# Four layers on one core: the second layer's second-half inputs and its gate z computed with the moving operand of both halves of x at once

## The reference

```python
proj = rmsnorm(x, norm_g) @ w_in
xc, zc, qd, kd, vd, zd, a_pre, b_pre = split_cols(proj, OD_SIZES)   # 1024 columns each
xconv = causal_dwconv(xc, conv_c_w) + conv_c_b                      # 4 taps along the tokens
yc = rg_lru(xconv, gate_w, gate_b, lam) * silu(zc)                  # gated linear scan
q, k, v = split(silu(causal_dwconv(concat(qd, kd, vd), conv_d_w)))  # 8 heads of 128
od = gated_delta_chunkwise(l2norm(q), l2norm(k), v, beta, g)        # needs a triangular inverse per head
yd = rmsnorm(od, onorm_g) * silu(zd)
x = x + concat(yc, yd) @ w_out
```

## Time and profile before

| | |
|---|---|
| median of 3 runs | 1913.81 us (1913.79 to 1914.02) |
| the profiled execution's own time | 1913.21 us |
| its span, first to last instruction | 1911.3 us |
| busy: PE, PEld, DVE, ACT, POOL | 1901.8, 1636.2, 1219.0, 1012.4, 170.1 us |
| mean granted TensorE clock | 0.999 of full speed |

### The profile page before, as it was taken

How to read it: one execution, slowest core, us unless ns; L and a number is a source line. 1 busy time by engine, 2 the same in 40 slices (tenths; PEclk the granted TensorE clock), 3 DMA queues, 4 the chain that set the end, 5 groups by cost and what they waited for, 6 DMA issues and landing times.

```text
span 1911.3 us, 26221 instructions
## 1 busy us (share of the span) xinstructions
PE 1901.8 (100%) x10370; PEld 1636.2 (86%) x10370; DVE 1219.0 (64%) x1688; ACT 1012.4 (53%) x1574; POOL 170.1 (9%) x142
## 2 busy tenths in 40 slices
PE   9999999999999999999999999999999999999998
PEld 7888888888889998898888888888888888888886
DVE  6655655555566887687557888645555778754553
ACT  7434445664557765764543345556454344446643
POOL 0000000110011111100001211000000111100110
PEclk9999999999999999999999999999999999999999
DMA  9555545545554444444565554554555555555453
GB/s 351 193 178 187 176 158 187 170 165 183 179 180 157 157 151 161 149 147 163 178 198 190 191 178 166 183 176 158 181 179 188 190 186 174 164 185 171 162 199 133
DMA packets 95033, 340.25 MB, mean 178 GB/s; under 512 B 10704, under 2 KB 11472, under 8 KB 94784
## 3 DMA queue, kind: packets, MB, share of 16 engines
q1 hardware_dynamic: 93536, 333.92, 52.4%
q0 software_dynamic: 944, 3.61, 0.6%
q10 hardware_dynamic: 432, 1.06, 0.1%
HBM read 336.44 MB, written 2.10 MB: 177 GB/s over the span
## 4 chain that ended last, share of the span: by engine, by line
PE 100%; ACT 0%; DVE 0%; issue 0%
PE ACC L736 18%; PE ACC L738 18%; PE ACC L737 18%; PE ACC L741 9%; PE ACC L744 9%; PE ACC L743 5%; PE ACC L742 5%; PE ACC L749 2%; PE ACC L750 2%; PE ACC L751 2%; PE PM L852 1%; PE PM L867 1%; PE PM L905 1%; PE PM L889 1%; PE PM L890 1%; PE PM L888 1%
## 5 line engine op out<-in xcount | busy, mean ns | idle before, releaser
L1441 DVE TENSOR_TENSOR WL<-RAW,WH 128x1024 fp32r<-128x1024 f32 (+1 forms) x624 | 791.8, 1284 | 534.3 <-ACT WH L1075 533.1
L1075 ACT ACTIVATE WH<-RAW 128x1024 fp32r<-128x1024 f32 (+1 forms) x626 | 650.7, 1052 | 508.9 <-PE ACC L738 264.9
L736 PE MATMUL ACC<-WH,XHL 128*128 128x512 f32 x1012 | 402.3, 397 | 0.0
L738 PE MATMUL ACC<-WH,XHL 128*128 128x512 f32 x1012 | 394.3, 390 | 0.0
L737 PE MATMUL ACC<-WL,XHL 128*128 128x512 f32 x1012 | 394.0, 389 | 0.0
L741 PE MATMUL ACC<-XHL,WH 128*128 128x512 f32 x768 | 307.9, 401 | 0.1
L744 PE MATMUL ACC<-XHL,WH 128*128 128x512 f32 x768 | 303.8, 396 | 0.0
L738 PEld LDWEIGHTS ACC<-WH,XHL 128*128 128x128 f32 x1012 | 190.0, 188 | 40.1
L737 PEld LDWEIGHTS ACC<-WL,XHL 128*128 128x128 f32 x1012 | 190.2, 188 | 38.6
L736 PEld LDWEIGHTS ACC<-WH,XHL 128*128 128x128 f32 x1012 | 190.1, 188 | 38.3
L743 PE MATMUL ACC<-XHL,WL 128*128 128x256 f32 x768 | 213.7, 278 | 0.0
(11 more groups left out here) (368 smaller groups left out, 2367.4 us busy)
## 6 DMA issues: line engine op xcount, KB each, us to landing
RAW<-in_w SPq DMA_DIRECT2D x621, 512.0 KB, 3.3
X<-in_x SPq DMA_DIRECT2D x4, 512.0 KB, 11.8
RAW<-in_w SPq DMA_DIRECT2D x6, 256.0 KB, 4.8
Y<-in_xT SPq DMA_DIRECT2D x2, 512.0 KB, 10.1
S<-in_bias POOLq DMA_DIRECT2D x8, 128.0 KB, 2.6
S<-in_od_gate_w POOLq DMA_DIRECT2D x1, 1024.0 KB, 6.1
S<-in_final_norm POOLq DMA_DIRECT2D x1, 1024.0 KB, 7.5
out<-Y SPq DMA_DIRECT2D x2, 512.0 KB, 2.6
```

Source lines behind the costliest of these rows:

```text
L736: e.matmul(o, th, hi[:, kk, :], start=f, stop=False)
L738: m = e.matmul(o, tl, hi[:, kk, :], start=False, stop=l)
L1075: e.activation(hi, src, ACT.Copy).then_inc(s_hi)
L1441: e.tensor_tensor(lo, src, hi.bitcast(F32), ALU.subtract).then_inc(s_lo)
```

## The change

It makes five feat jobs of the second layer wide: qd, kd and vd of the second half (slots 25 to 48) join the "sum" kind, and zc becomes four jobs of kind "zc" whose evacuation is a reduction and a multiplication on DVE. The convolution chains of summed inputs from the third on move: "copied" to 2, "taps" to 3 and "silu" to 4 pieces after the job's end. The sigmoid, exp and tanh steps of the scan come one slot earlier, all eight roots at slot 81. The two silu evacuations of zd come four and two pieces later. gate_c and split_c follow the four zc jobs.

```diff
-SUMMED = (("qd", 0), ("kd", 0), ("xc", 0), ("xc", 1))
+SUMMED = (("qd", 0), ("kd", 0), ("qd", 1), ("kd", 1), ("vd", 1), ("xc", 0), ("xc", 1))
...
-    both(1, "zc", w, 1024, "feat", "zc")
+    wide(1, "zc", w, 1024, "zc")
...
+        for b, late in ((0, 4), (1, 2)):
+            ENDS[LAST[J_OF[1, "zd", b]] + late] = ENDS.pop(LAST[J_OF[1, "zd", b]])
...
-                    at, late = conv_ends(c, i), 0 if CONV[c] in SUMMED else i
-                    put(at + 1 + late, "copied", (c, i))
-                    put(at + 2 + 2 * late, "taps", (c, i))
+                    at = conv_ends(c, i)
+                    after = (1 + i, 2 + 2 * i, 3 + 2 * i) if CONV[c] not in SUMMED else (1, 2, 3) if c < 2 else (2, 3, 4)
+                    put(at + after[0], "copied", (c, i))
+                    put(at + after[1], "taps", (c, i))
                     if c < 6:
-                        put(at + 3 + 2 * late, "silu", (c, i))
+                        put(at + after[2], "silu", (c, i))
...
-                put(b1 + 74 + n // 2, "gate_lru", n, 1)
-                put(b1 + 78 + n // 2, "decay_lru", n)
-                put(b1 + 82 + n // 4, "root_lru", n)
+                put(b1 + 73 + n // 2, "gate_lru", n, 1)
+                put(b1 + 77 + n // 2, "decay_lru", n)
+                put(b1 + 81, "root_lru", n)
...
-                    put((b1 + 92, L(1, "zc", 1) + 1)[b] + i, "gate_c", (b, i))
-                    put((b1 + 93, L(1, "zc", 1) + 2)[b] + i, "split_c", (b, i))
+                    at = L(1, "zc", 2 * b + i) + ((5, 3), (2, 1))[b][i]
+                    put(at, "gate_c", (b, i))
+                    put(at + 1 + (b == 0), "split_c", (b, i))
...
-                e.wait_ge(s_evD, at_D(1, "zc", b) - 1 + i)
+                e.wait_ge(s_evD, at_D(1, "zc", 2 * b + i))
...
                 elif J.kind == "zc":
+                    z = two(ZC[:, 512 * (J.b % 2):512 * (J.b % 2) + 512])
                     e.wait_ge(s_mm, p + 1)
-                    if J.b:
-                        e.wait_ge(s_zg, 2)
-                    for i in range(2):
-                        e.tensor_tensor(two(ZC[:, 512 * i:512 * i + 512]), two(acc[i]), row2, ALU.mult).then_inc(s_evD)
+                    if J.b > 1:
+                        e.wait_ge(s_zg, J.b - 1)
+                    e.tensor_reduce(z, halves_of(j), AX, ALU.add).then_inc(s_evD)
+                    e.wait_ge(s_evD, D_AT[j] - 1)
+                    e.tensor_tensor(z, z, row2, ALU.mult).then_inc(s_evD)
```

## The result

| | before | after |
|---|---|---|
| median, us | 1913.81 | 1923.7 (1923.3 to 1924.8) |
| ratio, 95% interval | | 1.0053 [1.0042, 1.0064] |
| profiled execution, own time / span | 1913.2 / 1911.3 | 1924.8 / 1922.4 |

The change makes the kernel 9.9 us slower. I had said 4.7 us slower, 1918.5, with a range from 1910 to 1922: the side was right, the size half of what came, and the time lies above the range.

What follows compares the result with a forecast made beforehand. PE was taken as the bound, always busy, with DVE a second bound where work is added. -3.75 of pace + 7.0 before slot 50 + 1.6 at zc = +4.8 us; predicted 1918.5, range 1910 to 1922.

Steps and rivals of the forecast that it cites:

- The pace: Forty pieces in slots 25 to 48 and 81 to 96: fewer matmuls save 0.094 us each, -3.75 us in all.
- DVE before slot 50: Slots 28 to 47: 10.6 us more before level_x against a margin of 5.9, so PE waits 7.0 us.
- the collision: Slot 28: v's taps (vd) right after a reduction meet POOL's multiplication, 1.0 us; 1.0 taken for all collisions.
- ACT's wait for the clears: Half 0's inverse: POOL's multiplication of slot 36 comes ahead of its clears, delaying ACT's copy; 2.0 us, ends 0 and 2.8.
- What a wait costs: Before slot 50: PE's wait counted at its length, 10.6 - 5.9 + 2.25 = 7.0 us.
- zd's evacuation: ACT's moved silu of zd: two table loads saved, two added at slot 32; net nothing, ACT waiting for DVE anyway.
- zc on DVE: Slots 84 to 98: 3.6 us more on DVE against a margin of 2.9; PE waits 1.6 us at the first solve.
- B: Rival: no new wait of PE, extra work vanishes in DVE's lag, only pace counts: 1910.1 us; chance 0.23.
- C: Rival: half the extra DVE work falls into DVE's existing waits, PE waits some 4 us: about 1914; chance 0.20.
- D: Rival: the matmuls saved bring nothing, up to the whole -3.75 us goes, waits alone give 1922; chance 0.05.
- E: Rival: the later chains, meant to spare ACT waits for POOL, cost or give nothing; no chance stated.
- The gate weights: Later taps and earlier gate products use some 7 of 18 us to spare: no cost.

Runs made afterwards that it cites:

- vd_only: The kernel before with only v's second half as wide pieces, its chain 2, 3 and 4 slots behind each job: 1913.3 us, ratio 0.9997.
- early_zd: Changed kernel with the LRU's gates and decays a slot earlier and zd's second half evacuated at its last piece, slot 80: 1923.7 us.
- no_q: Changed kernel with the second halves of q, k and v as feat pieces again; zc wide and the other moves kept: 1916.4 us.
- chain_now: Changed kernel with copied, taps and silu of summed jobs back at 1, 2 and 3 slots after the job's end: 1930.2 us.
- q_only: The kernel before with only the second halves of q, k and v wide and their chains a piece later: 1921.2 us.
- clears_first: Changed kernel with GpSimd's three clears for half 0's inverse put ahead of its multiplication for slot 36: 1922.2 us.
- order2: Changed kernel with taps and silu of v's second half a slot later and norm_sq in slot 45 instead of 46: 1925.7 us.
- filled: Changed kernel with eight extra matmuls (1.8 us), their results unread, where PE waits at norm_sum of slot 49: 1923.9 us.
- zd_home: Changed kernel with zd's second half evacuated at slot 80 again, two ScalarE table loads more: 1928.2 us.
- zc_pool: The kernel before with zc wide, zd, gates and decays as in early_zd, and zc's product moved from DVE to GpSimd: 1914.8 us.
- zc_late: zc_pool with zc's last evacuation one slot later, behind the last subtraction of half 1's inverse: 1914.8 us.
- vd_zc_late: zc_late with v's second half wide as well: 1914.1 us, ratio 1.0001 to the kernel before.
- wait_added: The kernel before with two extra ScalarE copies (2.2 us) ahead of its copies for the last part of half 1's inverse: 1915.8 us.
- qd_wide: The kernel before with, of q, k and v, only q's second half wide, and zc wide with old slots for zd, LRU and roots: 1923.6 us.

## Why the prediction was wrong

*The pace: right.* I had 0.094 us a piece; vd_only shows 0.091, and where nothing waits the changed kernel gains 0.08 to 0.09 a slot (slots 36 to 45, 87 to 97).

*DVE before slot 50: right in kind, 0.8 short.* ACT's copies end at 698.16 + 1.73 = 699.89, which is 11.4 us later than in the kernel before once the shift of 0.9 is taken off; my sum was 10.6. The terms one by one: reductions 1.22, and the six taps of slot 47 took 2.44 right before the last part, as said. At slot 28 the taps took 3.48 us for 2.45, the collision of 1.0 as said:
```profile
623.86 3.48 DVE L1698 SCALAR_TENSOR_TENSOR S<-S,VC 128x255 f32<-128x255 f32 x6
...
624.09 1.40 POOL L1977 TENSOR_TENSOR S<-S,C 128x512 f32<-128x512 f32 x1 [12.00 <-DVE S L1476]
```
The multiplications of slots 36, 40 and 44 each hit a small step of the inverse:
```profile
658.72 1.34 DVE L1796 TENSOR_TENSOR SC<-SC,VC 128x256 f32<-128x256 f32 x1
...
674.71 1.32 DVE L1806 TENSOR_TENSOR SC<-SC 128x56 f32<-128x56 f32 x1
```
That is 1.3 us for 0.43 and, twice, for 0.23 to 0.25 (the next of its kind, at 676.57). All four are 4.1; with the 1.9 taken off for slot 40 as before, 2.2, where I had 1.0. Each of them cost 0.9 to 1.1; the count of 1.0 for all four, which I had named and not taken, gives 2.1. ACT's wait for the clears was 2.25 for 2.0. PE's loss at slots 30 to 34 was 3.4 for my 3.3 (2.4 of it as listed idle time).

*What a wait costs: wrong.* The step reads "PE waits 10.6 - 5.9 + 2.25 = 7.0 us" and goes into the sum as 7.0. I counted a wait at its length. Here PE's granted clock fell to its lower level (1.2 instead of 2.4 GHz) behind two waits of four. Slot 51 is 6.8 us late where my sum gives 4.75: 0.8 from DVE, 1.2 from level_x reached late at the lower clock. Behind the wait at slot 85 another 1.1 (slots 85 and 86 begin 3.99 us apart, for 2.88). My sum had no term for this.

*zd's evacuation: wrong, and left out.* "Net nothing, and in each place ACT waits for DVE anyway" is the step that failed. I asked what the two slots do to ACT's table loads, and not who waits for the accumulator; and that zc's jobs are half as long, so that the accumulator is asked for four pieces earlier, I did not see. It costs 2.0 us of wait and the 1.1 of clock at its place. Taking it away gives back less: in early_zd 2.5 us at slot 87 and 0.6 at slot 101, since DVE's lateness at slot 98 then shows in full. The table loads came out as said, 63 in both kernels.

*zc on DVE: right.* I had a wait of 1.6 at the first solve; it was 1.1, and 1.6 in no_q. Without a wait at slot 85, as my sum had it, it is 2.0 (early_zd).

*The gate weights, the loads, the second inverse:* no cost, as said.

So of the 5.4 us between my +4.8 and the +10.2 of the timeline, 3.1 lie at zd's accumulator with the clock behind it (2.0 + 1.1), 1.2 are the clock before level_x, 0.8 DVE's sum; the rest are tenths. Rivals B, C and D can be laid aside: PE had new waits, they were not half as long, and the matmuls saved did bring 11 ns each. My E was wrong, as chain_now shows.

Chain and windows had been read for margins and the margins were good to half a microsecond. The range was too narrow because it took in only the bounds of DVE's work, and none for what follows a wait or for an accumulator that comes free too late.

## What to carry to other kernels

When a job is made shorter in pieces, look at every step that frees an accumulator, not only at those that the change touches: the same evacuation slot can become late because the next user comes sooner. Make a table of margins (result ready, result asked for) and let a change add work only where it fits under the next one; one of the three, v's, did here, and gained what the pace promised (q's did not; k's alone was not tried). Price a wait of PE above its length: here 2 us of wait cost 2 or 3.5.

## What the runs showed of the hardware

That the clock falls after a wait of only 2 us was new to me, and that it need not. At delta_q a wait of 2.0 us left it at 1.00 in the changed kernel and brought it down in q_only, windows of 640 to 650 us in both, the changed kernel first:
```profile
640.00:650.00 10.00, 8.01 (x48) 6.92 (x47) 8.04 (x18) 6.58 (x12) 1.27 (x1) 1.00 0.33 106
640.00:650.00 10.00, 8.00 (x37) 6.82 (x36) 8.04 (x18) 6.60 (x11) 1.27 (x1) 0.83 0.30 106
```
The wait of 2.0 to 2.1 us at slot 85 stands in six traces: the clock falls behind it in two (the changed kernel, chain_now) and stays at 1.00 in four (no_q, clears_first, order2, filled). Of all 21 waits of PE between 1.8 and 2.1 us in the 17 traces, 9 have a fall with them and 12 have none, and the 3.2 us in zd_home have none either. Every fall between 590 and 890 us begins in a wait or at most 2.0 us behind one, and the five kernels whose waits there are at most 1.2 us long (before, vd_only, zc_pool, zc_late, vd_zc_late) have none. Length alone does not decide it: in q_only the clock fell again 2.0 us behind the wait of 0.55 us at norm_sum. Both outcomes seem to come in executions of one and the same kernel, by the two groups of times of wait_added. The Trainium skill (TensorE: Matmul & The Clock Gate, What's actually happening) says that the moment at which the gate switches isn't tied to the kernel and varies from run to run; the two groups of times of wait_added agree. The spread shows it as well: 1913.3 to 1914.6 for the kernel before, 1921.2 to 1924.6 for qd_wide.

The clears had a second way to make DVE late. Its copy at the end of the inverse's first part took 2.24 us, and ended with GpSimd's last memset:
```profile
660.30 2.24 DVE L1799 COPY SC<-VC 128x128 f32<-128x128 f32 x1
```
In the kernel before the same copy took 0.22 us. It took 2.24 or 2.25 in all seven traces in which it meets the memsets. In clears_first six taps lay beside the same memsets and took 2.46 us, as ever. So a memset stops this copy of DVE and not an operation on two tiles. The Trainium skill (SBUF — State Buffer, Who interferes with whom) has both: an operation on two SBUF inputs contends with GpSimd's reads alone, a copy in a two-port mode with any access; these rows agree. I had cited only the first half. Here it cost nothing more, as ACT waited for the same memsets, and DVE, free again at 663.83, still waited 1.1 us for ACT's next split.

What decides whether a given wait brings the fall these runs do not settle. Not tried were a version that keeps PE busy in every new wait at once, one that takes reductions off DVE before slot 34, and k's second half alone.
